# One-hots of the first expert pair on VectorE, and the next layer's first modulation piece run in three parts

## The reference, cut to what matters

```
m   = silu(cond) @ w_mod[l] + b_mod[l]        # 1024 -> 6144: shift, scale, gate, twice
h   = layer_norm(...) * (1 + scale) + shift
aff = sigmoid(h @ router_w)                   # 16 affinities; best group of 4, best 2 in it
gates = the two affinities, divided by their sum
hid = silu(h @ w_gate[e]) * (h @ w_up[e])     # 1024 -> 512, for each of 16 experts
y   = sum over e of gates[e] * (hid @ w_down[e])
x   = layer_norm(2**0.5 * x + gate * y)
```

## Time and profile before

| | us |
|---|---|
| median of 3 runs (lowest, highest) | 865.54 (863.39, 866.21) |
| profiled execution: its own time | 865.44 |
| its span, first to last instruction | 863.6 |
| TensorE busy / VectorE / ScalarE / GpSimd | 775.2 / 233.3 / 151.4 / 63.3 |
| TensorE waiting for w_gate/w_up transfers, in sum | 29.2 |
| bytes read from HBM, mean rate | 278.99 MB, 332 GB/s |

### The profile page before, as it was taken

How to read it: one execution, slowest core, us unless ns; L and a number is a source line. 1 busy time by engine, 2 the same in 40 slices (tenths; PEclk the granted TensorE clock), 3 DMA queues, 4 the chain that set the end, 5 groups by cost and what they waited for, 6 DMA issues and landing times.

```text
span 863.6 us, 9955 instructions
## 1 busy us (share of the span) xinstructions
PE 775.2 (90%) x3765; PEld 371.1 (43%) x3765; DVE 233.3 (27%) x531; ACT 151.4 (18%) x389; POOL 63.3 (7%) x126
## 2 busy tenths in 40 slices
PE   4799788999999998797899996999999999997794
PEld 1345444546543443243234644554744434442331
DVE  0004444445210100000345055455610110000046
ACT  0211332213200111011112113233311101110120
POOL 0000000001100011001000030000200001101000
PEclk9898799999999999999999996999999999999998
DMA  8989940189999999999999899521099999999971
GB/s 312 382 311 401 389 152 31 68 307 404 419 419 417 420 419 417 419 422 414 417 386 384 321 353 420 227 98 64 35 370 417 420 416 419 421 415 418 419 321 50
DMA packets 78525, 287.37 MB, mean 333 GB/s; under 512 B 6508, under 2 KB 12140, under 8 KB 62100
## 3 DMA queue, kind: packets, MB, share of 16 engines
q1 hardware_dynamic: 74452, 275.60, 80.6%
q10 hardware_dynamic: 2880, 7.03, 2.1%
q0 software_dynamic: 1152, 4.19, 1.2%
HBM read 278.99 MB, written 7.82 MB: 332 GB/s over the span
## 4 chain that ended last, share of the span: by engine, by line
PE 50%; SPq 30%; DMA 7%; DVE 7%; issue 2%; ACT 2%; POOL 1%; ACTq 0%; DVEq 0%
SPq L580 15%; PE bank L1001 10%; SPq L575 9%; PE bank L748 9%; PE bank L837 6%; DMA ring<-in_exp_w_up 5%; SPq L576 4%; PE bank L1035 4%; PE bank L785 3%; PE bank L675 3%; DMA ring<-in_w_mod 2%; PE bank L654 2%; PE bank L972 2%; PE bank L816 2%; PE bank L794 2%
## 5 line engine op out<-in xcount | busy, mean ns | idle before, releaser
L1001 PE MATMUL bank<-ring,arena 128*64 128x512 f32 x1024 | 231.4, 605 | 30.1 <-DMA ring<-in_exp_w_up 29.2
L1001 PEld LDWEIGHTS bank<-ring,arena 128*64 128x64 f32 x1024 | 75.4, 139 | 182.8 <-issue 151.3
L1035 PE MATMUL bank<-ring,arena 128*64 128x512 f32 x512 | 113.8, 596 | 5.9 <-DMA ring<-in_exp_w_down 4.9
L1542 DVE TENSOR_TENSOR arena<-bank,arena 128x256 f32<-128x256 f32 x32 | 13.6, 424 | 253.6 <-ACT arena L1697 253.6
L748 PE MATMUL bank<-ring,arena 128*128 128x512 f32 (+2 forms) x224 | 75.4, 499 | 1.1 <-ACT arena L1631 1.1
L1621 ACT ACTIVATE arena<-bank 128x512 f32<-128x512 f32 (+6 forms) x79 | 41.0, 539 | 159.2 <-PE bank L748 66.9
L1035 PEld LDWEIGHTS bank<-ring,arena 128*64 128x64 f32 x512 | 36.1, 137 | 71.9 <-issue 64.6
L972 PE MATMUL bank<-arena 128*128 128x128 f32 x512 | 62.2, 275 | 0.0
L837 PE MATMUL bank<-ring,arena 128*128 128x512 f32 x128 | 60.3, 605 | 0.0
L972 PEld LDWEIGHTS bank<-arena 128*128 128x128 f32 x512 | 59.6, 192 | 1.3 <-issue 1.0
L675 PE MATMUL bank<-ring,cwin 128*32 128x512 f32 x384 | 48.2, 652 | 10.8 <-DMA ring<-in_w_mod 10.8
(11 more groups left out here) (168 smaller groups left out, 610.5 us busy)
## 6 DMA issues: line engine op xcount, KB each, us to landing
ring<-in_exp_w_gate SPq DMA_DIRECT2D x64, 1024.0 KB, 19.8
ring<-in_exp_w_up SPq DMA_DIRECT2D x64, 1024.0 KB, 20.6
ring<-in_exp_w_down SPq DMA_DIRECT2D x64, 1024.0 KB, 25.0
ring<-in_w_mod SPq DMA_DIRECT2D x24, 2048.0 KB, 18.2
expert_rows<-arena ACTq DMA_DIRECT2D x12, 512.0 KB, 7.8
ring<-in_w_out_ab SPq DMA_DIRECT2D x2, 2048.0 KB, 20.6
ring<-in_w_in_c SPq DMA_DIRECT2D x2, 2048.0 KB, 23.8
ring<-in_w_out_c SPq DMA_DIRECT2D x2, 2048.0 KB, 12.9
```

What stands on the lines that cost most here:

```text
L1001: mm = nc.tensor.matmul(pb(key)[SLOTS * hf:SLOTS * (hf + 1), :], xeT[b][:, k * P + SLOTS * a:k * P + SLOTS * (a + 1)], w[:, :, k % 4, hf * ...
L1035: mm = nc.tensor.matmul(pb(key)[SLOTS * a:SLOTS * (a + 1), :], hp[:, c:c + SLOTS], w[:, a, kf % 2, hf * HALF:(hf + 1) * HALF], start=(kf = ...
```

## The change

Layer 0's routing issues the modulation piece of layer 1 in three parts: the bias product and chunk 0 in place of the three fillers, chunk 1 behind the positions, chunks 2 and 3 inside pair 0, between its two gate/up products. The piece moves from bank 4 to bank 3. ScalarE copies it out after its part of pair 0 instead of before the experts. Turning its columns and VectorE's `mod_ab` move to the end of the layer's experts, behind the last down product. VectorE writes the one-hots of pair 0 itself, right behind the addition that makes the positions; GpSimd begins with pair 1, and its loop is written out. In layer 1 one filler stands behind the positions in place of four.

```diff
--- before.py
+++ after.py
@@ -243,14 +243,15 @@
                         t.use(("hr", l, g, q), (1, 2, 3, 1)[2 * g + q])
                 t.use(("pos", l), 7)
                 if l == 0:
-                    t.use(("mod", 1, 0), 4)
-                    t.use(("modT", 1, 0), 6)
+                    t.use(("mod", 1, 0), 3)
                 for a in range(2):
                     t.use(("gu", l, a), 4 + a, N_PAIR)
                     t.use(("xe", l, a), a, N_PAIR)
                     t.use(("ye", l, a), 7 - 5 * a, N_PAIR - a)
                 t.use(("ye_end", l), 4)
                 t.use(("tp", l), 6, N_EXP)
+                if l == 0:
+                    t.use(("modT", 1, 0), 6)
                 t.use(("ohT", l), 3)
             for g in range(G):
                 for hf in range(2):
@@ -954,7 +955,11 @@
                 mm.then_inc(*fill(key))
                 turn_back(l)
                 key = ("pos", l)
-                keep_busy(key, 3)
+                if l == 0:
+                    next_modulation(0)
+                else:
+                    keep_busy(key, 3)
+                room(pe, key)
                 pe.wait_ge(s_ch, l + 1)
                 out = pb(key)
                 nc.tensor.matmul(out[:, 0:32], tri, chosen[:], start=True, stop=False, skip_group_check=True)
@@ -963,7 +968,32 @@
                 nc.tensor.matmul(out[:, 64:80], ones, chosen[:, 16:32], start=False, stop=True,
                                  skip_group_check=True).then_inc(*fill(key))
                 if l == 0:
-                    modulation(1, 0)
+                    next_modulation(1)
+                else:
+                    keep_busy(("xe", 1, 0), 1)
+
+            def next_modulation(part):
+
+                key = ("mod", 1, 0)
+                out = pb(key)
+                if part == 0:
+                    room(pe, key)
+                    nc.tensor.matmul(out[0:32, :], cst(C_BIAS + 32, 32, DEPTH * N_MOD), rows[0:DEPTH * N_MOD, :],
+                                     start=True, stop=False, skip_group_check=True)
+                for c in ((0,), (1,), (2, 3))[part]:
+                    n = index[("mod", 1, c)]
+                    pe.wait_ge(*got(n))
+                    w = block_ap(n)
+                    for k in range(KD):
+                        j = k % 4
+                        mm = nc.tensor.matmul(out[32 * j:32 * j + 32, :], cwin[:, k, 24 - 2 * c:56 - 2 * c],
+                                              w[:, k * HALF:(k + 1) * HALF],
+                                              start=(c == 0 and 0 < k < 4), stop=False, skip_group_check=True)
+                    mm.then_inc(*release(n))
+                if part == 2:
+                    nothing = tri[0:DEPTH * N_MOD, 0:1].to_broadcast([DEPTH * N_MOD, 32])
+                    nc.tensor.matmul(out[0:32, 0:2], nothing, rows[0:DEPTH * N_MOD, 0:2],
+                                     start=False, stop=True, skip_group_check=True).then_inc(*fill(key))
 
             def gather(out, onehot, chunks, width):
 
@@ -1049,6 +1079,8 @@
                 for a in range(2):
                     pe.wait_ge(*saved(("xe", l, a), p))
                 gate_up(l, 0, n, ri, p, b, n - 1 if j > 0 else None)
+                if (l, j) == (0, 0):
+                    next_modulation(2)
                 gate_up(l, 1, n + 2, ri, p, b, n + 1)
                 hidden_turned(l, 0, p, n + 3)
                 pe.wait_ge(s_oh, p + (N_PAIR * l + 2))
@@ -1092,14 +1124,15 @@
                     spread(l, hf, ye_sb, 0, False)
                 hidden_turned(l, 1, p)
                 down(l, p, n + 4, None, (("ye_end", l), None))
+                if l == 0:
+                    pe.wait_ge(*saved(("mod", 1, 0)))
+                    mod_columns(1, 0)
                 for hf in range(2):
                     pe.wait_ge(*(saved(("ye", l, 0), p) if hf == 0 else saved(("ye_end", l))))
                     spread(l, hf, ye_end, 1, True)
                 pe.sem_inc(blk_free[(n + 5) % RING], 1)
 
             def experts(l):
-                if l == 1:
-                    keep_busy(("xe", l, 0), 4)
                 pe.wait_ge(s_oh, N_PAIR * l + 1)
                 for g in range(G):
                     for q in range(2):
@@ -1107,9 +1140,6 @@
                 for h in range(2):
                     room(pe, ("xe", l, h), 0)
                     gather(pb(("xe", l, h)), oh[0], range(4 * h, 4 * h + 4), P).then_inc(*fill(("xe", l, h)))
-                if l == 0:
-                    pe.wait_ge(*saved(("mod", 1, 0)))
-                    mod_columns(1, 0)
                 pair(l, 0)
                 with pe.Fori(0, 2) as i:
                     for j in range(1, 4):
@@ -1494,6 +1524,11 @@
                 dve.wait_ge(*full(("pos", l)))
                 out = pb(("pos", l))
                 ch.then(V.tensor_tensor(pg[:, 0:2, :], w2, out[:, 0:32].rearrange("p (g e) -> p g e", g=G), ALU.add))
+                for a in range(2):
+                    for g in range(G):
+                        last = V.tensor_scalar(oh[0][:, g, SLOTS * a:SLOTS * (a + 1)], cst(C_IOTA, SLOTS),
+                                               pg[:, g, a:a + 1], None, ALU.is_equal)
+                last.then_inc(s_oh, 1)
                 V.tensor_reduce(cmax[:], out[:, 64:80], AX.X, ALU.max).then_inc(*drain(("pos", l)))
                 dve.wait_ge(*saved(("pos", l)))
                 V.tensor_copy(over[:], cmax[:]).then_inc(s_over, 1)
@@ -1560,8 +1595,6 @@
             def experts(l):
                 for g in range(G):
                     affine(l, 0, g, 1)
-                if l == 0:
-                    mod_ab(1, 0)
                 row_numbers(l)
                 for hf in range(2):
                     affine_done(l, 0, hf)
@@ -1574,6 +1607,8 @@
                 both_hidden(l, N_PAIR - 1, (0,))
                 rows_taken(l)
                 both_hidden(l, N_PAIR - 1, (1,))
+                if l == 0:
+                    mod_ab(1, 0)
 
             def overflow(l):
                 o = ov[l]
@@ -1741,6 +1776,8 @@
                 for h in range(2):
                     gathered(l, h, 0, 0)
                 pair(l, 0)
+                if l == 0:
+                    copy_out(("mod", 1, 0), mods[1][:])
                 with act.Fori(0, 2) as i:
                     for j in range(1, 4):
                         pair(l, j, i)
@@ -1811,8 +1848,6 @@
                 act.wait_ge(s_out, 64 if l == 0 else 96)
                 modulated(l, 1)
                 route(l)
-                if l == 0:
-                    copy_out(("mod", 1, 0), mods[1][:])
                 experts(l)
                 overflow(l)
                 if l == 0:
@@ -1853,9 +1888,8 @@
                 return last
 
             def slots(l, p, j):
-                Q.tensor_copy(cur, pg[:, :, bass.ds(p * 2, 2)] if not isinstance(p, int) else
-                              pg[:, :, 2 * p:2 * p + 2]).then_inc(s_pool, 1)
-                pool.wait_ge(s_pool, p + (N_PAIR * l + 1))
+                Q.tensor_copy(cur, pg[:, :, 2 * p:2 * p + 2]).then_inc(s_pool, 1)
+                pool.wait_ge(s_pool, p + (N_PAIR - 1) * l)
                 b, t = turn[("tp", l)]
                 pool.wait_ge(filled[b], p * 2 + (t - 4))
                 pool.sem_inc(s_tick, 1)
@@ -1867,10 +1901,7 @@
 
             def experts(l):
                 pool.wait_ge(*saved(("pos", l)))
-                with pool.Fori(0, 2) as i:
-                    for j in range(3):
-                        slots(l, i * 3 + j, j)
-                for p in (6, 7):
+                for p in range(1, N_PAIR):
                     slots(l, p, p)
                 pool.wait_ge(s_stored, 16 * N_AWAY * (l + 1))
                 pool.wait_ge(*room_for(back_n[l]))
```

## The result

Over 20 runs each, the median went from 866.1 to 871.58 us. The ratio of the two is 1.0052, with a 95% interval of 1.0032 to 1.0072, so the change costs 4.5 us (2.8 to 6.2). One execution of the changed kernel took 1589 us and is left out of the ratio; the median of the other 19 is 871.35 us. On the 865.54 us from which the forecast set out, the ratio makes 870.0 us: inside the forecast range of 864.0 to 870.8, 1.8 above the forecast of 868.2. The absolute median lies above that range.

The account below looks back on a forecast made before the run. Transfers were taken to bound layer 0, and a delay of the stream to reach layer 1 in full. From 865.44 us, +3.7 for the stream, +1.5 for the layer's end and −2.4 for layer 1 gave 868.2 us, range 864.0 to 870.8.

Parts of the forecast that it names:

- Rival 1: Layer 0: TensorE sets the stage, as the chain of waits says, giving 862.5 us; chance 0.12.
- The stream: Layer 0's transfers, delayed by loads held behind chunks 2 and 3: 3.7 us late (bounds 2.5 and 5).
- The restart: Layer 0: time from issuing a load into an empty queue until transfers flow again, taken as 1.9 us.
- the queue ran out: Layer 0: issued loads last until 218.7 us, and the next load is issued at 221.1.
- hole: Layer 0, inside pair 0: DMA engines without transfers until flow resumes at 223.0 us, 4.3 us long.
- the old dip: Layer 0, kernel before: transfer shortfall at 207 to 210 us, worth 0.65 us, which the change would close.
- The layer's end: End of layer 0: turns, VectorE's six operations and the flag's read delay the next chain by 1.5 us (0.9 to 2.0).
- the flag's read: End of layer 0, VectorE: overflow flag's load of 0.44 us plus an estimated 0.35 for register work and branch.
- Layer 1: Fewer fillers and VectorE's one-hots start the gather, and the whole stream, 2.4 us earlier (2.0 to 2.6).
- TensorE's side: Layer 0: the first gate/up product starts at 212.1 instead of 217.6 us, TensorE 5.5 us ahead.
- Modulation part 0 for three fillers: Layer 0's routing: bias product and chunk 0 cost 2.7 us against about 2.6 for the fillers; positions end 0.75 later.
- Rival 3: Layer 1: with fewer fillers the clock falls under the gather, the gain becomes a 1.3 us loss, 871.9 us; chance 0.08.

Follow-up runs that it names:

- before_fillers: Kernel before plus four filler products in layer 0 between the first gather and the first gate/up product; timed +1.6 us (−0.8 to 3.8) against before.
- early_chunks: Changed kernel with chunks 1, 2 and 3 together behind the positions, so no load is held; timed +0.2 us against before.
- late_chunks: Changed kernel with chunks 2 and 3 behind both gate/up products of pair 0; timed 9 us more than the changed kernel.
- after_again: Changed kernel timed and profiled once more, no edit; +4.3 us against before, median 872.01 us.
- no_bank_wait: Changed kernel with layer 0's third row copy through bank 4 in place of bank 3; timed +5.5 us (3.4 to 7.5) against before.
- fillers_kept: Changed kernel with layer 0's three fillers put back ahead of modulation part 0; timed +6.8 us (4.2 to 9.2) against before.
- four_fillers: Changed kernel with no load held and turns ahead of the last pair, plus four layer 1 fillers in place of one; timed +0.6 us against before.

## Why the prediction was right, and where its size was off

**The sign and the place of the loss were right.** Layer 0's stage is set by the transfers, not by TensorE, although the chain of waits stands on TensorE until 254 us. `before_fillers` delayed TensorE by 3.6 us and moved no block; `early_chunks` had it 8.6 us later than the changed kernel and the block 2.3 us earlier; `late_chunks` held two loads 6.9 us longer and lost 7.0 us. Rival 1 is refuted.

**The parts, in the first profile.** The stream: forecast 3.7 us late, measured 2.5 (248.7 − 246.2). The restart took 1.7 us (issue 221.60, effective flow from about 223.3), not 1.9, and the queue ran out near 219.5, not 218.7, while the issue came 0.5 later than forecast. That is a hole of 3.8 us, or 3.1 against the old dip of 0.65; the other 0.6 is within what the block varies by: 245.2 to 246.4 in the six profiles without a hole. The layer's end: forecast 1.5, measured 2.1. The turns cost 1.0, and the flag's read 1.1 in place of the 0.6 that the sum left to it, since I took 0.8 from the rows, and 1.34 passed between the sixth operation and the update. Layer 1: forecast 2.4, measured 2.24. The sum, +2.4, meets the span's +2.5, and was forecast as +2.8. TensorE's side was forecast closely too: the first product of pair 0 stood 5.5 us earlier from the common start, as worked out.

**What the profile does not show is the rest, +4.5 timed against +2.5.** The timed interval starts at 2.8, so the size of the forecast is at its edge and not ruled out. If there is a missed cost, the step to suspect is "Modulation part 0 for three fillers": it was priced at full clock, 2.7 against 2.6 us. Rival 3 had a clock that falls, but in layer 1; there the gather stood at 2.08 to 2.10 us in every profile with one filler. In layer 0 the fillers are what stands behind the fall of 198 us, and part 0 took their place. Of eight profiles with part 0 there and its wait, three had 1.2 GHz until 210 to 212 us, among them one of the changed kernel's two. In that profile (`after_again`) the positions begin 2.4 us later, take 0.85 longer and chunk 1 another 1.7, so that chunk 2 is released 5.0 us later, and the block comes 4.8 us later (253.5 against 248.7). With that the loss of 2.2 us from the common start would be one of 7.0. Three in eight of the one and five of the other make 4.0 us, inside the timed 2.8 to 6.2. Of four profiles with fillers there, none was late.

That estimate is worked out, not shown, and four records speak against it:

- Four against eight profiles do not prove that the fillers decide the clock's return.
- `no_bank_wait` was timed at +5.5, with the clock back by 206 us in both its profiles.
- The timed runs exceed the profile (end from the common start, against before) also where by that account nothing should be missing: by 1.9 us in `fillers_kept`, which has the fillers, and by 2.9 in `four_fillers`, which holds no load. One profile is one execution out of a spread of 9 us (866.5 to 875.5), and before spreads as widely (863.4 to 871.9).
- Each timed run has its mean granted clock. In the changed kernel the 9 runs at 0.956 or less have a median of 873.8 us, the 10 above it 869.8; in `after_again` it is 873.8 for 8 runs and 869.6 for 4. In the kernel before, timed beside `after_again`, it is 869.8 for 11 runs and 865.8 for 24. So a low mean clock goes with 4 us in both kernels, though the one before has no such hole, and at either clock the changed kernel is about 4.0 us above. By an estimate, ten more microseconds at half clock lower the mean over 866 us by 0.006, most of the 0.008 that lie between the two groups. If they cost the changed kernel alone another 4.8 us, its groups should lie further apart than those of before. As far as these few runs tell, they do not.

So the loss at equal mean clock is about 4.0 us. The parts above explain 2.4 of it. The other 1.6 us, which is no more than the timed interval is wide to either side, stay open, as does what decides the clock's return. What is shown is that a late clock occurs in layer 0's routing. In the one pair of profiles of the same kernel it went with a block 4.8 us later while loads were held; `early_chunks` had it too, with its block on time.

The loss itself was decided by two choices of place. Chunks 2 and 3 were worth 4.8 us and the turns 2.3, as medians of 12 runs each timed side by side, give or take about 1.7 us by the spread of those runs; with both mended, 7.1 us.

## What to carry to other kernels

When an in-order load queue reuses buffers, work that frees a buffer has a deadline: the time when the queued bytes run out, less a restart. Ask of every move past that deadline, and read it from the engines' bytes, since the chain of waits may name a compute engine while the transfers are full. One profile is also one execution: before reading a gap between a profile and the timed runs, look where its own time lies among them. And work at half clock is a risk for a deadline: where the granted clock is seen to fall, price a release at both clocks, and keep small serial work, the read of a flag included, in a place where its engine waits anyway.

## What the runs showed of the hardware that I had not expected

The granted clock in one stretch differs between executions of the same kernel: 0.95 from 202 to 206 us in one, 0.50 until 210 in the other, behind the same 32 products of 16 columns and the row turns, with TensorE listed busy in 4.00 of 4.00 us in the slower one. The modulation's chunk of 16 MATMULs takes 1.93 us at the one and 3.64 us at the other, while the gather behind it takes 3.84 in both: in the slower one it starts at 212.29 us, and the clock from 212 to 214 us is 0.93.

The mean granted clock of a whole run goes with its time whatever the edit: runs at 0.956 or less are 4.0 us longer in the median, in the kernel before and in the changed one alike.
